# Second attention of a two-block kernel: a pair's output products issued between the scores and the transposes of a TensorE step

## The reference

```
s = (einsum('bqhd,bkhd->bhqk', qn, k_nope)
     + einsum('bqhr,bkr->bhqk', qr, k_rope)) * scale
p = softmax(where(mask, s, -inf), axis=-1)
o = einsum('bhqk,bkhd->bqhd', p, v)
```

## Time and profile before

| | |
|---|---|
| median of three runs | 3103.1 us (3101.68 to 3105.4) |
| the profiled execution, measured time | 3104.57 us |
| its span in the trace | 3102.7 us |
| TensorE matmuls busy | 2937.4 us, 95% |
| TensorE weight loads busy | 2577.2 us, 83% |
| VectorE, ScalarE, GpSimd busy | 2253.4 (73%), 1454.7 (47%), 915.8 (30%) us |
| DMA, mean rate | 175 GB/s |
| mean granted TensorE clock | 0.98 |
| the second attention's 64 units | from 2546.8 us to 2678.1 us |

### The profile page before, as it was taken

The page is one execution under the profiler, slowest core; times in us unless marked ns, Lnnn a source line. Parts: engine busy times, 40 slices in busy tenths (PEclk is TensorE's granted clock), DMA queues, the critical chain, the costliest instruction groups (busy, mean ns, idle before and its releaser), DMA issues.

```text
span 3102.7 us, 48421 instructions
## 1 busy us (share of the span) xinstructions
PE 2937.4 (95%) x17673; PEld 2577.2 (83%) x17673; DVE 2253.4 (73%) x3938; ACT 1454.7 (47%) x2587; POOL 915.8 (30%) x528
## 2 busy tenths in 40 slices
PE   5998999998989999999999999899999998989998
PEld 3776679998988888888888788689999975789997
DVE  4767514999978787888888245469887676588886
ACT  3348433445973333333333334466555446565553
POOL 2420233674005444455554321031110240121110
PEclk9999999999999999999999999799999999999999
DMA  6720122455579999999998111026554330156561
GB/s 247 273 74 1 61 89 94 168 172 183 219 246 349 339 336 339 335 346 350 346 352 294 70 62 49 21 75 169 148 149 134 104 96 1 38 134 165 149 162 55
DMA packets 198354, 542.32 MB, mean 175 GB/s; under 512 B 16928, under 2 KB 74400, under 8 KB 193824
## 3 DMA queue, kind: packets, MB, share of 16 engines
q1 hardware_dynamic: 78048, 272.00, 25.3%
q0 software_dynamic: 50112, 159.47, 16.7%
q10 hardware_dynamic: 70016, 108.54, 10.4%
HBM read 500.10 MB, written 39.85 MB: 174 GB/s over the span
## 4 chain that ended last, share of the span: by engine, by line
PE 66%; issue 18%; ACT 5%; DVE 5%; POOL 3%; DMA 2%; ACTq 0%; POOLq 0%; DVEq 0%
PE ps L1446 17%; PE ps L1383 16%; PE ps L1733 13%; PE ps L1766 8%; PE ps L1117 6%; POOL w_lo L2662 3%; ACT arena L2221 2%; DMA arena<-w_modulation 2%; PE ps L1168 1%; ACT arena L2237 1%; PE ps L1495 1%; DVE arena L2741 1%; DVE arena L2792 1%; PE ps L1364 0%; PE ps L755 0%
## 5 line engine op out<-in xcount | busy, mean ns | idle before, releaser
L2662 POOL TENSOR_TENSOR w_lo<-ring,w_hi 128x1024 fp32r<-128x1024 f32 x164 | 420.5, 2569 | 1017.0 <-ACT w_hi L899 1016.8
L899 ACT ACTIVATE w_hi<-ring 128x1024 fp32r<-128x1024 f32 x364 | 381.8, 1054 | 445.2 <-PE ps L1446 235.9
L1446 PE MATMUL ps<-w_hi,arena_r 128*128 128x512 f32 x1536 | 426.9, 397 | 4.5 <-DVE arena_r L3147 4.5
L1383 PE MATMUL ps<-h_hi,w_hi 128*128 128x384 f32 x1024 | 355.5, 347 | 5.2 <-issue 5.2
L1446 PEld LDWEIGHTS ps<-w_hi,arena_r 128*128 128x128 f32 x1536 | 288.8, 188 | 72.4 <-DVE arena_r L3147 5.2
L1383 PE MATMUL ps<-h_lo,w_hi 128*128 128x384 f32 x1024 | 348.9, 341 | 0.0
L1383 PE MATMUL ps<-h_hi,w_lo 128*128 128x384 f32 x1024 | 346.3, 338 | 0.0
L3136 DVE TENSOR_TENSOR w_lo<-ring,w_hi 128x1024 fp32r<-128x1024 f32 x188 | 228.2, 1221 | 135.2 <-ACT w_hi L899 133.3
L2675 POOL DMA_INDIRECT arena<-u_rows,arena x128 | 192.9, 1507 | 376.6 <-DVE arena L3123 355.7
L2675 POOL DMA_INDIRECT arena<-v_rows,arena x128 | 206.4, 1612 | 175.0 <-DVE arena L3129 143.9
L1446 PE MATMUL ps<-w_lo,arena_r 128*128 128x512 f32 x768 | 241.8, 397 | 0.0
(11 more groups left out here) (381 smaller groups left out, 7189.5 us busy)
## 6 DMA issues: line engine op xcount, KB each, us to landing
ring<-weight_stream SPq DMA_DIRECT2D x460, 512.0 KB
gates<-arena ACTq DMA_DIRECT2D x12, 2048.0 KB, 7.3
arena<-gates ACTq DMA_DIRECT2D x32, 768.0 KB, 14.5
arena<-ffn_out SPq DMA_DIRECT2D x36, 512.0 KB, 4.2
arena<-w_modulation ACTq DMA_DIRECT2D x17, 1024.0 KB, 7.3
early_acts<-arena ACTq DMA_DIRECT2D x64, 192.0 KB, 3.1
arena<-early_acts ACTq DMA_DIRECT2D x32, 384.0 KB
arena<-weight_stream SPq DMA_DIRECT2D x44, 256.0 KB, 3.2
```

Of the source, the lines that this page charges most:

```text
L899: act.activation(w_hi[:, s, :], ring[:, s, :], ACT.Copy).then_inc(hi_ready, 1)
L1383: last = pe.matmul(ps[:, bank, 0:ND], w, v, start=c == 0 and p == 0, stop=c == DC - 1 and p == 2)
L1446: last = pe.matmul(ps[:, Y_BANKS[b][half], :], a[u], w[v][:, half * BANK:(half + 1) * BANK], start=first and p == 0, stop=final and p == 2)
L2662: pool.tensor_tensor(w_lo[:, s, :], ring[:, s, :], w_hi[:, s, :], ALU.subtract)\
```

## The change

In TensorE's list of the second attention the call of `m_out` moves ahead of the call of `m_turn` within a step. The instructions, their operands and their semaphores' counts stay as they are; the lists of the other engines aren't touched.

```
@@ -1952,10 +1952,10 @@
                     m_meta_out()
                 if u == 3:
                     pe.wait_ge(meta_act, DIFF_META_ACTS + 3)
+                if u >= 4 and u % 2 == 0:
+                    m_out(u - 4)
                 if 2 <= u < n + 2:
                     m_turn(u - 2)
-                if u >= 4 and u % 2 == 0:
-                    m_out(u - 4)
```

## The result

The changed kernel took 3116.04 us as median of 11 runs (3109.49 to 3121.07), the kernel before 3105.4 us (3100.56 to 3109.05) beside it. The ratio is 1.0032, interval [1.0024, 1.0041]: slower by 9.9 us, between 7.5 and 12.7. A second set of runs gave 1.0038 [1.0025, 1.005].

The account below looks back on a forecast made before the run. The bound was taken to be a loop of waits: odd scores, maximum, exponential, keep, output products. Transposes' 11.9 us plus 2.1 us for bank 7's copies made 14.0 us more, forecast 3117 us, range 3109 to 3125.

Parts of the forecast that it names:

- the sum: Second attention stage: 11.9 us for transposes plus 2.1 us for bank 7's copies, 14.0 us slower in all.
- The loop goes through the keep: Odd scores, maximum, exponential, ScalarE's keep, output products, next odd scores set the pace; products can't start earlier, transposes join the loop.
- The transposes' price: Transposes now stand between products and next odd scores on TensorE: 0.21 to 0.55 us a step, 11.9 us in all.
- Bank 7's copies: ScalarE's copies at head pair ends finish 0.3 us after the next exponential is due, at seven ends: 2.1 us.
- The clock: Rival, chance 0.12: added idle lowers TensorE's clock for 4 us in each of eight periods, 12 us more, 3129 us.
- The gain of 11 us: Rival, chance 0.06: products fill TensorE's 11.0 us wait before transposes, giving 3092.1 us.
- No change: Rival, chance 0.10: VectorE or ScalarE takes up the shift in the stage, giving 3103 to 3109 us.
- Pass-through: Outside the stage, no cover was counted behind it or at the front, so the 14.0 us reaches the end.

## Why the prediction was right

The forecast was 3117 us in 3109 to 3125 with 0.85 on slower. The measured median is 3116.04, or by the ratio 9.9 us above before; the stage alone lost 13.5 us, for the 14.0 of the sum. The mechanism was right. That the number came within 1 us is in part luck: the 14.0 us added lie outside the measured 7.5 to 12.7, and the forecast stood on three runs whose median, 3103.1 us, is 2.3 below that of the kernel before in the comparison. Inside the stage, too, one term was too large and a fall of the clock that the sum left out made up for most of it.

- *The loop goes through the keep.* Right: the products start 0.05 us behind the keep's end after as before, though the transposes' wait for the normalisation was gone. The transposes left out or doubled move the changed order's period by 1.3 and 1.1 us; in that of before leaving them out moves nothing. Too strong was that they lie beside the loop, with nothing but the keep to hold the products: the earlier trace rows show that for one of the four places of a period, and at the three others the transposes would have let the products go only 0.03 to 0.12 us sooner (see the doubled transposes).
- *The transposes' price,* 11.9 us. The distances are 0.60 and 0.27 us with four blocks and one, each 0.05 to 0.06 more than taken from the earlier trace rows, so 13.6 us. But the scores now follow transposes and not products, and their maximum starts 0.45 us after them (2595.99 to 2596.44) where it was 0.56: 0.10 us less in each of 30 loops, 3.0 us. (Per period: 0.27 + 0.38 + 0.49 + 0.60 - 4 x 0.10 + 0.29 for bank 7's copies = 1.63 = 17.12 - 15.49.) The term should have been 10.6 us. The exchange of the two neighbours was priced at their own lengths alone; what follows each had to be counted too.
- *Bank 7's copies,* 2.1 us. The exponential would have been due 0.25 us behind the start of its bias (L3612: 0.15 us and 0.10 to ScalarE, as from 2596.78 to 2597.03), at 2600.98 + 0.25 = 2601.23, and starts at 2601.52, directly behind the second copy: 0.29 us, seven times 2.0. Right.
- *The clock.* Both kernels have one fall in the first 10 us of the stage. The changed one has a second in its first period, behind a 1.71 us wait, in both of its profiles, for about 1.0 us (the products of three and of four blocks start 4.96 and 4.90 us apart there, 3.96 later); this is in the 13.5 and not in the sum. 10.6 + 2.0 + 1.0 = 13.6. After that the clock held 1.00 through the 1.71 us waits of the changed kernel. By the rule of the Trainium skill that stood in the prediction (TensorE: Matmul & The Clock Gate, section A second HAM failure mode: psum-queue depth-cycling), frequent short idle times between groups of matmuls can make the clock swing. The changed kernel disagrees from its second period on, but its neighbour with the products ahead of the four-block transposes only, and the one with doubled transposes, agree: 1.05 us lost in every full period, and 0.8 to 1.5 in four of six. The rival with 0.12 priced a fall in each of eight periods; one came here, but kernels that differ by a few instructions have it in all. A fall cost 1.05 us, for the 4 x 0.36 = 1.44 expected. One reading was wrong: the earlier trace rows were said to put a fall under 8 us, but a mean of 0.51 over 8 us means that this one lasted nearly all of them.
- *The gain of 11 us* by filling the transposes' wait is not to be had with products that wait for the keep themselves. With the products of a pair whose keep is over it is, and about twice that: some 21 us. *No change* fell with the stage's 13.5 us.
- *Pass-through.* The stage's 13.5 us, less the 0.8 to 1.5 us by which the part behind it was shorter in the profiles, is 12 to 12.7; the ratios say 9.9 (7.5 to 12.7) and 11.8 (7.8 to 15.5). The difference isn't resolved by these runs.

## What to carry to other kernels

A wait in front of an instruction is worth filling only with work that is ready then: look up what the filler itself waits for, and whether that ends later. If the filler's wait is already the link that closes the loop, everything that it is moved ahead of joins the loop. The cure was to issue the filler one step or two later, when its inputs were long there; the four buffers that the kernel has were enough, and the same order within a step went from 10 us slower to about 21 us faster. And one place of a period doesn't speak for the others: at each, look for a second path that ends just ahead of the one that holds.

## What the runs showed of the hardware

- The same 1.71 us wait, with the same matmuls behind it, left the clock at 1.00 in every period of the changed kernel but the first, and took it to 0.50 in every full period of a kernel whose other steps had the old order, in two of two executions. With transposes left out the clock also fell in the order of before, in four of seven periods (mean 0.89 to 0.97), though none of TensorE's waits between the units there was over 1.2 us. No run here shows which difference decides.
- Products for 64 columns directly behind transposes start 0.10 us later than scores for 128 columns do (in the variant one step later and behind, from the start of the transposes to that of the products 2600.51 to 2600.88 with one block: 0.37 us, against 0.27 to scores in the changed kernel), and the scores behind such products give their result 0.10 us later (the maximum starts 0.56 us behind their start, against 0.45 behind transposes). Where the products had to wait anyway, the first is hidden.
